# Two transformer blocks on one core: another order of work in the up chunks of the SwiGLUs, and most of the query projection moved into the attention of the second block

## The reference, cut to what matters

```python
def swiglu(x, w_gate, w_up, w_down):
    return (jax.nn.silu(x @ w_gate) * (x @ w_up)) @ w_down
...
def ada_norm(h, g, shift, scale):
    return rms_norm(h, g) * (1 + scale) + shift
...
def mla_q(cq, g_qn, w_uq, cos, sin):
    bsz, t, _ = cq.shape
    q = (rms_norm(cq, g_qn) @ w_uq).reshape(bsz, t, N_HEADS, QK_NOPE + QK_ROPE)
    if cos is None:
        return q
    q_nope, q_rope = q[..., :QK_NOPE], q[..., QK_NOPE:]
    return jnp.concatenate([q_nope, apply_rope(q_rope, cos[:, None, :], sin[:, None, :])], axis=-1)
...
    # in each of the two layers of the second block
        h = h + HALF * gt1 * swiglu_2(ada_norm(h, g_ffn1[l], sh1, sc1), w1_ffn1[l], w3_ffn1[l], w2_ffn1[l])
        ...
        attn = attend_blocked(q_lat, jnp.concatenate([k_ctx, k_lat], axis=1),
                              jnp.concatenate([v_ctx, v_lat], axis=1))
        y = merge_branches(u, conv_module(...), attn @ w_o_mla[l], fourier_mix(...), ...)
        h = h + gt2 * y
        h = h + HALF * gt3 * swiglu_2(ada_norm(h, g_ffn2[l], sh3, sc3), w1_ffn2[l], w3_ffn2[l], w2_ffn2[l])
```

## Time and profile before

| | |
|---|---|
| median of 3 runs | 3067.95 us (3062.25 to 3068.5) |
| the profiled execution | 3072.34 us |
| its span, first to last instruction | 3070.6 us |
| mean granted TensorE clock | 0.980 of 2.4 GHz |
| busy share of the span: PE, PEld, DVE, ACT | 95%, 86%, 67%, 45% |
| read from HBM | 482.66 MB, 158 GB/s |

### The profile page before, as it was taken

How to read it: one execution, slowest core, us unless ns; L and a number is a source line. 1 busy time by engine, 2 the same in 40 slices (tenths; PEclk the granted TensorE clock), 3 DMA queues, 4 the chain that set the end, 5 groups by cost and what they waited for, 6 DMA issues and landing times.

```text
span 3070.6 us, 52038 instructions
## 1 busy us (share of the span) xinstructions
PE 2925.6 (95%) x19700; PEld 2633.2 (86%) x19700; DVE 2065.1 (67%) x3317; ACT 1372.1 (45%) x2219; POOL 138.2 (4%) x205
## 2 busy tenths in 40 slices
PE   8998998998999999999899999999999999899998
PEld 8887998887999988898677898888988889779998
DVE  4657785657777777778764365767667667776665
ACT  5555445554545432354544254222542225645443
POOL 0000000000000000010000020100201002000000
PEclk9999998998999999999999999999999999999999
DMA  6435664434665565452212344544546445226454
GB/s 235 145 113 169 240 235 157 145 110 158 206 212 185 186 228 194 158 183 81 71 45 79 110 172 151 204 153 169 192 144 217 146 151 169 90 63 190 150 189 140
DMA packets 147700, 486.21 MB, mean 158 GB/s; under 512 B 16320, under 2 KB 25792, under 8 KB 147392
## 3 DMA queue, kind: packets, MB, share of 16 engines
q1 hardware_dynamic: 126640, 407.22, 39.9%
q0 software_dynamic: 20880, 76.56, 7.3%
HBM read 482.66 MB, written 1.05 MB: 158 GB/s over the span
## 4 chain that ended last, share of the span: by engine, by line
PE 78%; DVE 11%; ACT 5%; issue 4%; DMA 2%; DVEq 0%; POOLq 0%; ACTq 0%; SPq 0%; POOL 0%
PE bank L1857 21%; PE bank L1858 21%; PE bank L1859 21%; DVE wlo L1071 4%; ACT whi L570 3%; PE bank L1801 3%; PE bank L1802 2%; PE bank L1803 2%; PE aux L2057 1%; DVE acc L1589 1%; PE bank L2075 1%; PE bank L1932 1%; PE aux L2161 1%; DVE bbb L1141 1%; PE aux L2064 1%
## 5 line engine op out<-in xcount | busy, mean ns | idle before, releaser
L1857 PE MATMUL bank<-uhi,whi 128*128 128x256 f32 (+1 forms) x4000 | 1246.4, 312 | 12.2 <-DVE wlo L1071 8.3
L1071 DVE TENSOR_TENSOR wlo<-raw,whi 128x1024 fp32r<-128x1024 f32 (+4 forms) x850 | 948.9, 1119 | 451.1 <-ACT whi L570 445.9
L1858 PE MATMUL bank<-ulo,whi 128*128 128x256 f32 (+1 forms) x4000 | 1229.3, 307 | 0.0
L1859 PE MATMUL bank<-uhi,wlo 128*128 128x256 f32 (+1 forms) x4000 | 1229.2, 307 | 0.0
L570 ACT CAST whi<-raw 128x1024 fp32r<-128x1024 f32 (+4 forms) x850 | 810.2, 961 | 290.4 <-PE bank L1859 193.2
L1857 PEld LDWEIGHTS bank<-uhi,whi 128*128 128x128 f32 x4000 | 757.4, 189 | 76.5 <-issue 20.6
L1858 PEld LDWEIGHTS bank<-ulo,whi 128*128 128x128 f32 x4000 | 754.3, 189 | 46.9 <-issue 3.1
L1859 PEld LDWEIGHTS bank<-uhi,wlo 128*128 128x128 f32 x4000 | 754.2, 189 | 44.2
L1857 PE MATMUL bank<-yhi,whi 128*128 128x256 f32 (+1 forms) x1432 | 442.5, 309 | 20.2 <-DVE wlo L1071 13.6
L1858 PE MATMUL bank<-ylo,whi 128*128 128x256 f32 (+1 forms) x1448 | 440.9, 304 | 0.0
L1859 PE MATMUL bank<-yhi,wlo 128*128 128x256 f32 (+1 forms) x1432 | 435.5, 304 | 0.0
(11 more groups left out here) (265 smaller groups left out, 2940.4 us busy)
## 6 DMA issues: line engine op xcount, KB each, us to landing
raw<-in_w_stream SPq DMA_DIRECT2D x674, 512.0 KB, 3.5
big<-in_w_ada POOLq DMA_DIRECT2D x64, 512.0 KB, 3.9
vt<-in_w_ada POOLq DMA_DIRECT2D x51, 512.0 KB, 3.7
raw<-in_w_stream SPq DMA_DIRECT2D x80, 256.0 KB, 2.7
raw<-in_w_stream SPq DMA_DIRECT2D x48, 384.0 KB, 3.1
bbb<-in_w_ada POOLq DMA_DIRECT2D x29, 512.0 KB, 3.8
raw<-in_w_stream SPq DMA_DIRECT2D x32, 192.0 KB, 2.3
raw<-in_w_stream SPq DMA_DIRECT2D x16, 128.0 KB, 2.0
```

The lines of the kernel that those rows point to most:

```text
L1071: ve.tensor_tensor(wlo[:, u % SLOTS, 0:n], raw[:, u % SLOTS, 0:n], whi[:, u % SLOTS, 0:n].bitcast(F32), ALU.subtract).then_inc(s_low, 1)
L1857: te.matmul(out_, whi[:, u % SLOTS, w], hi(k)[:, c0:c1], start=k == 0, stop=False)
L1858: te.matmul(out_, whi[:, u % SLOTS, w], lo(k)[:, c0:c1], start=False, stop=False)
L1859: ins = te.matmul(out_, wlo[:, u % SLOTS, w], hi(k)[:, c0:c1], start=False, stop=k == plan.kt[u] - 1)
```

## The change

There are two parts.

In every up chunk ScalarE now rounds the coming weights ahead of its eviction, with or without a `then`. VectorE now makes, for unit j, the product, then `low(j+3)`, then the remainder of the product's tile, and then the modulation sums (in that order for every chunk; `late` holds the last two). Streams that aren't up chunks keep their order.

Of the 8 query units only the first 2 (layer 0) or 4 (layer 1) stay ahead of the attention. The others run inside it, two for each step: TensorE at the steps 0, 1 and 2 (layer 0) or 0 and 1 (layer 1), behind the scores of that step, in the banks 0 and 1 by turns; ScalarE's copies and VectorE's rotary operations one step later.

```diff
+        self.first = 2 if l < L - 1 else 4
+        self.queries = {j: (j - self.first) // 2 for j in range(self.first, H)}
...
                 if then is not None:
                     for j in range(n):
+                        if ahead:
+                            high(u0 + j + AHEAD)
                         evac(j % per, j // per)
-                        high(u0 + j + AHEAD)
+                        if not ahead:
+                            high(u0 + j + AHEAD)
                         then(j)
...
-                stream(u0, plan.count[name], 4, evac, then=then, ahead=name[-1] != "0")
+                stream(u0, plan.count[name], 4, evac, then=then, ahead=True)
...
                 for n in range(N + 1):
                     if n < N:
                         turned2(n)
+                    for j in heads.queries_at(n - 1):
+                        query(l, j, pair(U[f"q{l}"], j))
+                        high(U[f"q{l}"] + j + AHEAD)
...
                         evac(j % per, j // per)
                         low(u0 + j + AHEAD)
+                        late(j % per, j // per)
                         then(j)
...
                         ve.tensor_tensor(hid(k)[:, c0:c1], sg(k)[:, c0:c1], bank(u0, j)[:, c0:c1],
                                          ALU.mult).then_inc(read(u0, j), 1)
+
+                def late(j, i):
+                    k = j // 2
+                    if j % 2:
                         ahi.wait(1)
                         t = 2 * i + (tile + k)
                         rest(lo[:, t, c0:c1], hid(k)[:, c0:c1], hi[:, t, c0:c1])
                     if name in plan.ada:
                         ada(name, j, i)
-                stream(u0, plan.count[name], 4, evac, [(ahi, 2)], then, ahead=name[-1] != "0")
+                stream(u0, plan.count[name], 4, evac, [(ahi, 2)], then, late=late)
...
+                    for j in heads.queries_at(n - 1):
+                        rope(l, j)
+                        low(U[f"q{l}"] + j + AHEAD)
...
+                    for j in heads.queries_at(n):
+                        query(l, j, True)
                     for k in heads.units_at(n):
                         unit4(k)
...
-                for j in range(H):
-                    unit(u0, j, 0, 0, lambda k: yhi[:, qt_[k], :], lambda k: ylo[:, qt_[k], :], c0, T2)
-                pe.wait_ge(*after(u0 + H - 1))
+                first = Heads(l).first
+                for j in range(first):
+                    query(l, j, False)
+                pe.wait_ge(*after(U[f"q{l}"] + first - 1))
```

More of the change, by code:

```diff
@@ L214, in units_at, with queries_at @@
         return [k for k, at in self.places.items() if at == n]
+    def queries_at(self, n):
+        return [j for j, at in self.queries.items() if at == n]
     def closes(self, n):
@@ L876, in ffn2, with query @@
                 hidden2(up + "2", 0 if before is not None else S, T2)
+            def query(l, j, from_):
+                c0, u0 = S if l == L - 1 else 0, U[f"q{l}"]
+                done(u0, j, 0, 0)
+                sc.copy(big1[0:QK, j, c0:T2], from_[0:QK, c0:T2])
+                sc.copy(swapped[j // 2][:, j % 2 * S:(j % 2 + 1) * S], from_[QK:P, S:T2]).then_inc(read(u0, j), 1)
             def attention2(l):
@@ L1023, in _ @@
                                 bank(u0, j)[:, :].rearrange("p (t c) -> p t c", t=2)).then_inc(read(u0, j), 1)
-                u0 = U[f"q{l}"]
-                for j in range(H):
-                    high(u0 + j + AHEAD)
-                    done(u0, j, 0, 0)
-                    sc.copy(big1[0:QK, j, c0:T2], bank(u0, j)[0:QK, c0:T2])
-                    sc.copy(swapped[j // 2][:, j % 2 * S:(j % 2 + 1) * S],
-                            bank(u0, j)[QK:P, S:T2]).then_inc(read(u0, j), 1)
+                for j in range(Heads(l).first):
+                    high(U[f"q{l}"] + j + AHEAD)
+                    query(l, j, bank(U[f"q{l}"], j))
                 attention2(l)
@@ L1072, in low, with stream @@
                                  whi[:, u % SLOTS, 0:n].bitcast(F32), ALU.subtract).then_inc(s_low, 1)
-            def stream(u0, n, per, evac, tallies=(), then=None, ahead=False):
+            def stream(u0, n, per, evac, tallies=(), then=None, ahead=False, late=lambda j, i: None):
                 iters = n // per
@@ L1089, in body @@
                             low(u0 + j + AHEAD, i, per)
+                        late(j, i)
                 repeat(dve, iters - 1, body, tallies)
@@ L1097, in stream @@
                         low(u0 + n - per + j + AHEAD)
+                    late(j, iters - 1)
             def done(u0, j, i, per):
@@ L1595, in taps, with rope @@
                         self.at += 1
+            def rope(l, j):
+                if j % 2:
+                    bcast = lambda t: t.unsqueeze(1).to_broadcast([ROPE, 2, S])
+                    dve.wait_ge(*after(U[f"q{l}"] + j))
+                    qx = big1[HD:QK, j - 1:j + 1, S:T2]
+                    sw = swapped[j // 2].rearrange("p (a t) -> p a t", a=2)
+                    step.add(ve.tensor_tensor(qx, qx, bcast(cos), ALU.mult))
+                    chained(ve.tensor_tensor(sw, sw, bcast(sin), ALU.mult))
+                    ve.tensor_tensor(qx, qx, sw, ALU.add).then_inc(s_dop, 1)
             def attention2(l, conv):
@@ L1734, in _ @@
                     conv.taps(2)
-                u0 = U[f"q{l}"]
-                bcast = lambda t: t.unsqueeze(1).to_broadcast([ROPE, 2, S])
-                for j in range(H):
-                    low(u0 + j + AHEAD)
-                    if j % 2:
-                        dve.wait_ge(*after(u0 + j))
-                        qx = big1[HD:QK, j - 1:j + 1, S:T2]
-                        sw = swapped[j // 2].rearrange("p (a t) -> p a t", a=2)
-                        step.add(ve.tensor_tensor(qx, qx, bcast(cos), ALU.mult))
-                        chained(ve.tensor_tensor(sw, sw, bcast(sin), ALU.mult))
-                        ve.tensor_tensor(qx, qx, sw, ALU.add).then_inc(s_dop, 1)
+                for j in range(Heads(l).first):
+                    low(U[f"q{l}"] + j + AHEAD)
+                    rope(l, j)
                 attention2(l, conv)
@@ L2045, in ffn2, with query @@
                 stream(U[up + "2"], 2 * CHUNKS2[2], 4, u2h, u2l, c0, T2)
+            def query(l, j, paired):
+                qt_ = [2, 3, 8]
+                unit(U[f"q{l}"], j, 0, 0, lambda k: yhi[:, qt_[k], :], lambda k: ylo[:, qt_[k], :],
+                     S if l == L - 1 else 0, T2, paired)
             def attention2(l):
```

3 lines of the change are left out of this document (removed).

## The result

| | before | changed |
|---|---|---|
| median (lowest to highest) of 9 runs each | 3069.15 us (3062.25 to 3078.42) | 3047.43 us (3034.79 to 3056.07) |
| profiled execution, span | 3070.6 us | 3033.0 us |

The ratio is 0.9924, 95% interval 0.9908 to 0.994: 23 us less, between 18 and 28. The forecast was 22 us less. The changed kernel's profiled execution happens to be the fastest of the nine, and the two profiles differ by 37.6 us, so some 14 us of what they differ by isn't the change. What these are comes behind the waits.

A forecast was written before the change was run, and what follows sets the result against it. PE, busy 95% of the span, was taken to bound the kernel, through its waits and slow clock. Terms of 9 + 4 + 3.5 + 1 + 4.5 = 22 us gave 3046 us, range 3036 to 3058 (over 0.8).

The forecast's parts named there:

- Term 1: Seams at fup200c and fup110c: shorter two-engine loop, shorter PE waits, clock partly back; 9 us, from 7 to 11.
- Term 2: up10: weights' remainder now ahead of the modulation sums, so PE stops waiting for it; 4 us, from 0 to 4.4.
- Term 3: fup100c: weights wait goes, squares wait shrinks, a new wait comes at the spread; 3.5 us of 7.6 at most.
- Term 4: fup100 and up12: waits below 1 us for weights; 1 us, from 0 to 1.5.
- The costs of the new order are hidden, as far as rows go: Up chunks: later remainders of weights and of the last tile still end before PE or the down stage needs them.
- Term 5: Query projection to first gate unit: 2.5 us in layer 0, 2 in layer 1; 4.5 us, from 0 to 8.
- What goes is the idle DVE and PE of the steps that follow: Attention, term 5: the longest wait, 3.0 us, stays; the gain is idle time in the steps behind it.
- The waits only move: Rival: waits left in seams and attention start drop the clock as longer ones did; 13 us, 3055; chance 0.22.
- Slower: Rival: weights' remainder, tied to the product in up chunks, comes too late, PE waits each pair in up01; 3090; chance 0.04.

The follow-up runs named there:

- Apply first: On the changed kernel: in fup200c and fup110c VectorE makes each tile's apply but the first ahead of the weights' remainder; 3033.81 us, ratio 0.9885 to before.
- DVE half: On the kernel before: only VectorE's part of the up chunks' reorder, ScalarE and queries as before; 3084.51 us, ratio 1.0025.
- Sums early: On the changed kernel: modulation sums at units 0 and 1 of four instead of 0 and 2, in chunks with one modulation row; 3025.69 us, ratio 0.9859 to before.
- ACT half: On the kernel before: only ScalarE's rounding of coming weights ahead of the eviction in every up chunk, VectorE and queries as before; 3055.13 us, ratio 0.9929.
- reorder only: The changed kernel with the query move undone, up chunks in the new orders; 3046.72 us, ratio 0.9903 to before.
- query move only: The kernel before with only the query move, up chunks as before; 3073.46 us, ratio 0.999.
- query under the wait: On the changed kernel: first two moved query units ahead of the first transposition, layer 0's first rotary turn behind two maxima; 3045.94 us, ratio 0.9925 to before.

## Why the prediction was right, and where it wasn't

The total was right (22 us forecast, 23 measured), but it was partly luck: terms 1 and 3 gave 7 us more than forecast and terms 4 and 5 some 6 less.

- **Term 1, seams: 9 us, measured 11.5** (76.9 to 70.5, 75.5 to 70.4), a little above its upper end. The loop of 6.7 us came out at 6.60, the spread's wait went, 1.6 us stood at the first pair (1.9 forecast), and 2.4 and 3.4 at the second in the two profiles. Apply first shows the mechanism: with the loop cut, neither pair waits. What I didn't see is that VectorE's half alone makes the loop longer, and that ScalarE's alone brings only the first seam's gain.
- **Term 2, up10: 4 us, measured 3.8** (4.6 and 3.0 for first and second profiles, 3.0 over all eight). The mechanism named holds in part: VectorE still waits for the data, longer than before, and PE's waits for remainders fell to 1.0 us in one profile but stayed at 3.0 in the other (2.9 and 3.6 before). The remainder's place alone doesn't bring it, since the DVE half left up10 at 87.3 us, and the sums' place alone does, with 81.3 us on before.
- **Term 3, fup100c: 3.5 us, measured 7.9.** This is the mis-sized term. It assumed "1 to 2 us" of a new wait at the spread; there was none, and the clock stayed at 1.00. That wait does come where only the clock stays up: in the second profile of before the 1.9 us wait for weights had PEclk 1.00 behind it, and then PE waited for the spread:

```profile
PE aux L1842 <- DVE pt L1264: 1.7, 1, 1.7
```

So the order of ScalarE and VectorE took it out. I take it that the root's chain gained as much as TensorE did, since ScalarE's roundings stand in it too; no run tried that alone. The ACT half alone brought 7 of it.
- **Term 4, small ones: +1 us, measured -3.0** (-0.9, -1.2 and -0.9 in up00, up12 and fup100 with their down stages; over all eight profiles 1.4, -1.0 and -3.4). The step that failed is "The costs of the new order are hidden, as far as rows go". It followed each queue for one pair of units, and not the buffer of the modulation, whose load is issued by the sum that moved behind a remainder. Sums early shows it: with one unit more for the load, these stages come out 4.0, 0.5 and 5.8 us under before. Most of that was to be had without the change (3.2, 0.2 and 4.6 us with the same edit on before); what is left beside it is a gain of 0.2 to 1.2 us a stage, as small as the term's. In down12 the wait was for the last tile's remainder, which I had called hidden because that tile is read over 2 us on; the whole queue was late by then.
- **Term 5, query: 4.5 us, measured 2.7.** To the first gate matmul 2.5 and 2.8 us came out, as forecast, but in layer 0 not by the way forecast. "What goes is the idle DVE and PE of the steps that follow" failed there: PE was as idle as before (4.3 and 4.2 us), and what changed is the clock: at PEclk 0.86 up to 5.0 of the 35.5 us were lost to it, at 0.95 up to 1.7 of the 33.0. The prediction had counted the clock only as the risk of this term. In layer 1 PE's idle time did fall, but it was given back behind the first gate matmul: from there to bm1 it took 73.6 us before and 76.7 after, with PE idle for 6.8 instead of 4.0 us, 3.6 instead of 1.8 of it for the scaling. I had stepped both queues only to the first gate matmul, where the stretch that had to be shortened went on.
- **Rivals.** "The waits only move" was right in that VectorE's wait for data, which this rival didn't name, grew in four stages, and mostly wrong on the seams: both got shorter by 5 to 6 us, though the clock still fell behind the second in one profile of two. "Slower" didn't come in up01. Its mechanism (the remainder too late) is real in the DVE half, where up12 with its down stage took 58.2 us instead of 51.4: VectorE waited there 14.0 us for ScalarE's roundings of weights (4.8 before) and only 0.4 for data.

What stays open: why the load takes 6.3 us from issue to landing in the changed up00 (3.9 and 5.6 in the two profiles of before). That it stands behind two loads of weights isn't shown: when it was issued, mostly one of them was under way, and so it was in before and in sums early. Nor is it that all loads are slower: with the sums early those of weights took a median of 4.2 us in up00, as in the changed kernel, and those of the modulation 3.8.

## What to carry to other kernels

When an operation is moved back in a queue, ask which buffers it frees and when their loads are issued: the wait turns up an iteration later, at a DMA, on an engine that isn't the bound. Where two engines hand work to and fro in a loop, reordering one may lengthen the loop that reordering both shortens, and elsewhere one half may be all of the gain, so test the halves. And follow a stall that is taken out to the end of the stage, since the engine that paces the stage takes it back there.

## What the hardware showed that I hadn't expected

**Two spacings of one matmul.** At PEclk 1.00 and with PE never idle, matmuls of 256 columns start each 0.1133 or each 0.1177 us, and a stage keeps its level until TensorE has waited or changed its work. The level differs between executions of one program (43.5 and 45.2 us for the same 384 matmuls), which sums to 8 us between the two profiles of before. So two profiles mustn't be subtracted before such stages are set aside. The Trainium skill (TensorE: Matmul & The Clock Gate, "Part 1: The HAM clock gate") gives matmuls back to back at the full clock a spacing of the columns by 2.4 GHz plus 2.5 ns; for 256 columns that is an estimate of 0.109 us. Both levels here lie above it, in a kernel where each matmul has a weight load of its own; the measurements decide.

**Which wait costs the clock is a draw, within bounds.** Waits of TensorE ahead of fup200l or fup110l, and the PEclk of the 8 us behind, from the profiles of before and changed, two each, reorder only, query move only, both halves, query under the wait and sums early (apply first, and the kernels with it, have no such wait):

| wait, us | PEclk behind |
|---|---|
| 1.6 (three times) | 1.00 |
| 1.9 | 0.79 |
| 2.2, 2.3 | 1.00 |
| 2.3, 2.4, 2.8 | 0.79 |
| 3.4 | 1.00 once, 0.79 once |
| 4.0 to 4.6 (nine times) | 0.63 to 0.79 |

None of 1.6 us cost anything, and each of 4 us or more did: 0.79 means 42% of 8 us at 1.2 GHz, 1.7 us lost, and 0.63 means 3.0. Between them it goes either way at one and the same length. The wait of 1.9 us in fup100c does so within one program: 0.79 behind it in the first profile of before, 1.00 in the second. The same section of the Trainium skill says that the point of transition depends on where in a free-running window the work falls, and the trace agrees as far as equal waits had different clocks behind them.
